# Key pages of a paged decode cache: strips of 32 partitions and block transposes on VectorE, two sequences per score

## The chip, the cores and the metric

The kernel runs on one core of a Trainium2 chip. The metric is the device time of one execution in microseconds (us), the median of several runs; lower is better. The engines are named as in the profile: PE (TensorE, its weight loads as PEld), DVE (VectorE), ACT (ScalarE), POOL (GpSimd) and SP (SyncE, which here only issues DMAs). PSUM is the memory that PE writes, in eight banks of 512 float32 per partition.

## What is computed

One step of a two-layer decoder, all in float32: a prompt of 1,024 new positions, and 8 sequences that add 4 positions each to a cache of 4,096 past positions. Layer A mixes by a convolution module, layer B by stick-breaking attention; each ends in a gated feed-forward network. The change touches the attention alone:

```python
z = jnp.einsum('bqhd,bkhd->bhqk', qb, kb) * scale + bias_f
causal = s_pos[None, :] < t_pos[:, None]
log_one_minus = jnp.where(causal, jax.nn.log_sigmoid(-z), 0.0)
after = lax.cumsum(log_one_minus, axis=3, reverse=True) - log_one_minus
w = jnp.where(causal, jnp.exp(jax.nn.log_sigmoid(z) + after), 0.0)
o = jnp.einsum('bhqk,bkhd->bqhd', w, vb)
...
past_k = cache_k[page_table].reshape(bs, -1, N_HEADS, HEAD_DIM)
past_v = cache_v[page_table].reshape(bs, -1, N_HEADS, HEAD_DIM)
```

There are 16 heads of 64. The weight of a key is sigmoid(z) times the product of sigmoid(-z) over all later keys, so keys are taken from the newest to the oldest and a running product ("remainder") is carried. A page holds 128 positions of all heads: 512 KB of keys and 512 KB of values. The 8 sequences have 32 pages each, 256 in all, scattered over a pool and named by a table.

## The kernel before

The stages follow one another: layer A, its feed-forward network, keys, values and queries of the new positions, the attention stage (`mix_sp`, `mix_pe`, `mix_act`, `mix_dve`, `mask_pool`, lines 2151 to 2622), then the output projection and the second feed-forward network. Weight tiles stream from HBM through three buffers (`raw`); ACT and DVE split each into a high and a low part (`split_hi` L369, `split_lo` L374), and PE makes three products per block (L1146).

The attention stage is a loop of 132 phases, written out by hand for each engine; semaphores tie the engines together. In phase p of the first 128:

- Two key pages are turned. SP loads each as 128 partitions (positions) by 1,024 columns (head, feature) of 4 KB into a ring of six (`kr`, L2197). PE turns every page in eight 128x128 transposes (L2262) into two PSUM banks of the four `TURN_BANKS`; ACT copies one half to `kt` (L2432), DVE the other (L2519). `kt` then has 128 rows (two heads of 64 features) for each of eight head pairs.
- In every odd phase a chunk of four pages (`CP = 4`, 512 positions of one sequence) is scored: eight products of 512 columns (L2275) from `kt` and the queries `qst`, which stand at places of their own among zeros. A sequence has 16 heads x 4 queries = 64 rows of the 128. ACT makes the two sigmoids (L2438, L2443), DVE the running product (`page_remainders`, a scan of 512, L2530) and the weights (`page_weights`, L2539). Three phases after the scoring PE turns the weights (L2284) and, a phase later, multiplies them with the value pages (`page_outputs`, L2298), which SP loads into a ring of six (`vr`).
- In three phases of four a unit of the prompt's own attention goes through the same steps for one pair of heads, 128 queries and up to 512 keys: scores (L2317), sigmoids (L2460, L2470), scan (L2564), mask on POOL (L2188), weights (`prompt_weights`, a product on DVE, L2576), transposes (L2327) and values (L2336). Seven of the eight pairs are scored in three products of rounded high and low parts (made by `pair_high` on ACT and `pair_low` on POOL, L2177), the first pair in one float32 product. Keys, queries and values of a pair come by three DMAs (`load_pair`, L2223 to L2225) every 16 phases.

SP's program in the loop alternates: read a page number from the table (`value_load`, L2193), wait until the ring has a free place, issue the key page; the same for a value page eight pages behind (`V_LAG`). A place in `kr` is free when PE has turned the page (`s_th`), one in `vr` when PE has summed it (`s_pv`). In the last phases PE makes six of the eight blocks of the first output-projection tile (`attention_product`, L1301) between other work.

## Time and profile before

| | us |
|---|---|
| median of 3 runs | 3069.11 |
| lowest and highest run | 3067.57, 3071.78 |
| the profiled execution, its own time | 3068.7 |
| its span, first to last instruction | 3067.0 |
| attention stage, first page transpose to last | 1449.8 to 2174.4 |

The profile is one execution. Busy time of an engine is the time in which it has an instruction under way; idle time is put down to what ended it. "PEclk" or the granted clock is 1.00 at the full level (2.4 GHz) and 0.50 at the lower (1.2 GHz). "DMA share" is the time that the packets of all 16 DMA engines took, over 16 times the stretch, each packet booked where it starts, so that it can pass 1; GB/s are their bytes. GB/s divided by the share is what the engines move when all are busy.

### The profile page before, as it was taken

What the parts mean: (1) busy time and instruction counts of PE and PEld (TensorE: products, weight loads), DVE (VectorE), ACT (ScalarE), POOL (GpSimd) and SP (SyncE); (2) the same over time, 40 slices, a digit from 0 to 9 for tenths busy, and PEclk for the clock granted to TensorE, in tenths of its full rate; (3) what the DMA queues carried; (4) which work ended last, traced back from release to release, by engine and by line L of the source; (5) the groups of instructions that cost most, each with busy time, mean ns of one, the idle gap of its engine ahead of it and who ended that gap; (6) DMA issues with size and microseconds to landing.
All of it is one profiled execution on the core that took longest, in us unless ns stands there. A gap on an engine that the chain in (4) does not pass through costs nothing. (4 is left out here: it accounts for less than half of the span.)

```text
span 3067.0 us, 60298 instructions
## 1 busy us (share of the span) xinstructions
PE 3028.2 (99%) x23786; PEld 2606.3 (85%) x23786; DVE 1983.1 (65%) x2953; ACT 1387.2 (45%) x2363; POOL 251.7 (8%) x412
## 2 busy tenths in 40 slices
PE   8999999999999999999999999999999999999998
PEld 7987888888999998998666777676788888999998
DVE  6998677745655345534878888878667763565522
ACT  5444633333333333323777777777543333333322
POOL 0212000000000002221111111111000000000000
PEclk9999999999999999999999999999999999999999
DMA  4222233334333335647999999999633333333332
GB/s 131 76 82 79 82 96 96 96 107 120 103 91 90 97 104 184 192 146 228 356 391 384 383 386 383 392 394 376 233 102 96 97 95 112 111 110 90 88 107 86
DMA packets 483243, 534.49 MB, mean 174 GB/s; under 512 B 22241, under 2 KB 400474, under 8 KB 482888
## 3 DMA queue, kind: packets, MB, share of 16 engines
q1 hardware_dynamic: 467254, 482.90, 46.8%
q0 software_dynamic: 15616, 47.55, 4.6%
q8 instruction: 190, 3.11, 0.4%
q14 instruction: 91, 0.75, 0.1%
q10 hardware_dynamic: 92, 0.19, 0.0%
HBM read 486.84 MB, written 33.89 MB: 170 GB/s over the span
## 5 line engine op out<-in xcount | busy, mean ns | idle before, releaser
L377 DVE TENSOR_TENSOR wlo<-raw,whi 128x1024 fp32r<-128x1024 f32 (+1 forms) x368 | 441.9, 1201 | 556.7 <-ACT whi L372 543.4
L372 ACT CAST whi<-raw 128x1024 fp32r<-128x1024 f32 (+1 forms) x368 | 379.5, 1031 | 916.7 <-PE PS L1146 878.5
L1146 PE MATMUL PS<-xfh,whi 128*128 128x512 f32 (+2 forms) x2240 | 618.8, 327 | 1.2 <-DVE wlo L377 0.9
L1146 PE MATMUL PS<-xfh,wlo 128*128 128x512 f32 (+2 forms) x2240 | 615.1, 326 | 0.0
L1146 PE MATMUL PS<-xfl,whi 128*128 128x512 f32 (+2 forms) x2240 | 613.5, 325 | 0.0
L1146 PEld LDWEIGHTS PS<-xfh,whi 128*128 128x128 f32 x2240 | 379.0, 188 | 35.9 <-issue 3.8
L1146 PEld LDWEIGHTS PS<-xfl,whi 128*128 128x128 f32 x2240 | 379.7, 188 | 32.3 <-issue 0.5
L1146 PEld LDWEIGHTS PS<-xfh,wlo 128*128 128x128 f32 x2240 | 378.4, 188 | 32.8
L2262 PE MATMUL PS<-ident,kr 128*128 128x128 f32 x2048 | 276.9, 276 | 2.3 <-ACT kt L2432 2.3
L2262 PEld LDWEIGHTS PS<-ident,kr 128*128 128x128 f32 x2048 | 225.5, 140 | 50.3 <-issue 49.4
L2519 DVE COPY kt<-PS 128x512 f32<-128x512 f32 x256 | 169.1, 675 | 87.2 <-PE PS L2262 85.3
L1146 PE MATMUL PS<-pZ,whi 128*128 128x512 f32 x640 | 197.4, 390 | 0.0
L1601 DVE TENSOR_SCALAR cv<-gx,fT 128x512 f32<-128x512 f32 (+1 forms) x132 | 49.4, 402 | 197.2 <-issue 190.6
L1146 PE MATMUL PS<-pA,whi 128*128 128x272 f32 x1024 | 171.4, 289 | 0.0
L2432 ACT COPY kt<-PS 128x512 f32<-128x512 f32 x256 | 152.4, 596 | 40.7 <-PE PS L2262 38.9
L1146 PEld LDWEIGHTS PS<-pA,whi 128*128 128x128 f32 x1024 | 145.0, 188 | 0.6 <-issue 0.5
L1605 DVE SCALAR_TENSOR_TENSOR cv<-gx,fT,cv 128x512 f32<-128x512 f32 (+1 forms) x264 | 142.4, 581 | 3.1
L1146 PEld LDWEIGHTS PS<-pZ,whi 128*128 128x128 f32 x640 | 120.1, 188 | 24.9
L1543 ACT ACTIVATE gel<-cv 128x512 f32<-128x512 f32 (+1 forms) x88 | 56.8, 646 | 183.5 <-DVEq L1612 183.4
L949 DVE SCALAR_TENSOR_TENSOR mT<-u,vec,mT 128x513 f32<-128x513 f32 (+1 forms) x203 | 135.9, 746 | 4.3 <-ACT mT L856 4.3
L2298 PE MATMUL PS<-vr,wT 128*32 128x256 f32 x2048 | 136.8, 385 | 1.5 <-DVE PS L2587 1.5
L2275 PE MATMUL PS<-kt,qst 128*32 128x512 f32 x1024 | 123.1, 595 | 7.7 <-issue 6.3
(379 smaller groups left out, 5311.3 us busy)
## 6 DMA issues: line engine op xcount, KB each, us to landing
kr<-in_cache_k SPq DMA_DIRECT2D x256, 512.0 KB, 6.7
vr<-in_cache_v SPq DMA_DIRECT2D x256, 512.0 KB, 6.4
raw<-in_ffn_w_gate SPq DMA_DIRECT2D x88, 512.0 KB, 3.7
raw<-in_ffn_w_up SPq DMA_DIRECT2D x88, 512.0 KB, 3.7
raw<-in_ffn_w_down SPq DMA_DIRECT2D x64, 512.0 KB, 3.9
raw<-in_ffn_w_down SPq DMA_DIRECT2D x32, 384.0 KB, 3.5
raw<-in_conv_w_glu SPq DMA_DIRECT2D x16, 512.0 KB, 4.0
raw<-in_conv_w_out SPq DMA_DIRECT2D x16, 512.0 KB, 3.9
```

The source lines that it names most:

```text
L372: nc.scalar.copy(whi[b][:, 0:blocks_of(t), :], raw[t % RAWS][:, 0:blocks_of(t), :]).then_inc(w_hi, 1)
L377: nc.vector.tensor_tensor(wlo[t % RAWS][:, 0:n, :], raw[t % RAWS][:, 0:n, :], whi[b][:, 0:n, :].bitcast(F32), ALU.subtract).then_inc(w_lo, 1)
L949: glu_then(nc.vector.scalar_tensor_tensor(out=d, in0=src, scalar=w, in1=d, op0=ALU.mult, op1=ALU.add))
L1146: mm = nc.tensor.matmul(PS[:, s + c, 0:c1 - c0], stationary(wt, t, kw + k), x(k0 + k)[:, c0:c1], start=start and k == 0 and wt is whi and ...
L1543: nc.scalar.activation(gel[:, 0:w], cv[0][:, 0:w], ACT.Gelu_apprx_tanh).then_inc(f_gel, 1)
L1601: then(nc.vector.tensor_scalar(a_, win(0), tap, None, ALU.mult))
L1605: then(nc.vector.scalar_tensor_tensor(out=d, in0=win(j), scalar=tap, in1=s_, op0=ALU.mult, op1=ALU.add))
L2262: mm = nc.tensor.transpose(PS[:, bank, j * P:(j + 1) * P], kr[slot][:, a * P:(a + 1) * P], ident[:])
L2275: mm = nc.tensor.matmul(PS[32 * g:32 * g + 32, 2, :], qst[:, c // SEQ_CHUNKS, a, :], kt[:, a, :], start=e == 0, stop=e == 1, skip_group_ch ...
L2298: mm = nc.tensor.matmul(PS[32 * g:32 * g + 32, 3, 0:256], wT[c % 2][:, m, 32 * g:32 * g + 32], vr[slot][:, 256 * g:256 * g + 256], start=F ...
L2432: nc.scalar.copy(kt[:, 0:4, m * P:(m + 1) * P], PS[:, turn_bank("page", x, 0), :].rearrange("p (a s) -> p a s", a=4)).then_inc(s_ka, 1)
L2519: nc.vector.tensor_copy(kt[:, 4:8, m * P:(m + 1) * P], PS[:, turn_bank("page", x, 1), :].rearrange("p (a s) -> p a s", a=4)).then_inc(s_kd, 1)
```

## The change

Key pages are no longer turned by PE. Two pages at a time, one of each of two sequences, are loaded in strips: for each page two DMAs (`f` = 0, 1), each with half of the features (512 columns) into 32 partitions, as four rows of 2 KB per partition. The four strips of a step fill 128 partitions. DVE then turns the step in two instructions of 1,024 elements, in 32x32 blocks, from `kr` straight to `kt`. `kt` has 32 rows for each of (feature half f, sequence z), and 16 blocks; a chunk is two steps (`CP = 2`), 256 positions of two sequences, so scores have 128 useful rows: sixteen products of 256 columns instead of eight of 512. There are still 64 chunks, 256 pages and 128 phases; scans, sigmoids and weights of a chunk are 256 wide instead of 512.

Also: the prompt's weight product moves from DVE to POOL; all prompt pairs are scored in one float32 product, so `pair_high` and `pair_low` go; the prompt's outputs have bank 7 to themselves and `TURN_BANKS` are three; the new positions' keys and queries come by eight strip DMAs and are put in place by 20 small copies (before: two DMAs, four copies); the first output-projection tiles are split after the loop, and none of their blocks is made inside it.

```diff
-KR, VR = 6, 6
+KT, VR = 3, 6
-CP = 4
+CP = 2
+DP = DB // 2
+SC = CP * PAGE
...
+    kr = [stack(f"kr{j}", [P, 4, 512]) for j in range(KT)]
...
-    sp.dma_start(kTs[:], k_dram[:, :, NP:T].rearrange("a p t -> p a t")).then_inc(s_in, 16)
-    sp.dma_start(qTs[:], q_dram[:, :, NP:T].rearrange("a p t -> p a t")).then_inc(s_in, 16)
+    for raw_, dram in ((kraw, k_dram), (qraw, q_dram)):
+        for q0 in range(4):
+            f = q0 // 2
+            src = dram[4 * f:4 * f + 4, :, NP:T].rearrange("a (j n) t -> n (a j) t", n=32)
+            sp.dma_start(raw_[32 * q0:32 * q0 + 32, :, :], src).then_inc(s_in, 16)
...
 def mask_pool(pool):
     for u, (pr, i, kc) in enumerate(ATT):
...
+            pool.wait_ge(a_r, 2 * u + hh + 1)
+            if u >= 1:
+                pool.wait_ge(t_full, turns["prompt", u - 1, hh] + 1)
+            nc.gpsimd.tensor_tensor(wq[hh][:, 0:w], beta[hh][:, 0:w], rem[hh][:, c0 + 1:c0 + 1 + w], ALU.mult).then_inc(a_w, 1)
...
-def load_page(sp, x, cache, ring, landed, freed, each):
-    number = sp.value_load(ptab[0:1, page_entry(x):page_entry(x) + 1], min_val=0, max_val=cache.shape[0] - 1)
-    slot = x % len(ring)
-    if x >= len(ring):
-        sp.wait_ge(freed, each * (x - len(ring) + 1))
-    sp.dma_start(ring[slot][:], cache[ds(number, 1)].rearrange("a s h d -> (a s) (h d)")).then_inc(landed[slot], 16)
+def load_k_page(sp, x):
+    number, step, z = page_number(sp, x, A["cache_k"]), x // 2, x % 2
+    if step >= KT:
+        sp.wait_ge(s_th, 2 * (step - KT + 1))
+    page = A["cache_k"][ds(number, 1)].rearrange("a s h d -> (a s) (h d)")
+    for f in range(2):
+        q0 = 64 * f + 32 * z
+        sp.dma_start(kr[step % KT][q0:q0 + 32, :, :],
+                     page[:, 512 * f:512 * f + 512].rearrange("(c r) n -> r c n", c=4)).then_inc(s_k[step % KT], 16)
...
 def page_scores(c):
-    pe.wait_ge(s_ka, CP * (c + 1))
-    pe.wait_ge(s_kd, CP * (c + 1))
+    pe.wait_ge(s_th, 4 * c + 4)
...
-    for e in range(2):
+    for i in range(4):
         for g in range(4):
-            a = 2 * g + e
-            mm = nc.tensor.matmul(PS[32 * g:32 * g + 32, 2, :], qst[:, c // SEQ_CHUNKS, a, :], kt[:, a, :],
-                                  start=e == 0, stop=e == 1, skip_group_check=True)
+            mm = nc.tensor.matmul(PS[32 * g:32 * g + 32, 2, 0:SC], qst[:, c // SEQ_CHUNKS, 4 * g + i, :], kt[:, 4 * g + i, :],
+                                  start=i == 0, stop=i == 3, skip_group_check=True)
...
-    terms = ((qp, kp),) if pr == 0 else ((qh, kh), (qh, kl), (ql, kh))
...
 for p in range(PHASES):
-    if pages:
-        page_half_turned(pages[0], 0)
     if turned is not None:
         prompt_weights_turned(turned, 0)
-    if pages:
-        page_half_turned(pages[0], 1)
     if summed is not None:
         page_weights_turned(summed)
-    if pages:
-        page_half_turned(pages[1], 0)
-        page_half_turned(pages[1], 1)
...
-    if p >= PHASES - 4 and p < PHASES - 1:
-        j = p - PHASES + 4
-        attention_product(pe, 0, 2 * j, 2 * j + 2)
...
-attention_product(pe, 0, 6, KB)
+attention_product(pe, 0, 0, KB)
...
+def page_turned(p, h):
+    c, m, slot = p // CP, p % CP, p % KT
+    if h == 0:
+        dve.wait_ge(s_k[slot], 64 * (p // KT + 1))
+        if c >= 1 and m == 0:
+            dve.wait_ge(s_sc, c)
+    nc.vector.transpose(bass.AP(kt, m * P + 64 * h, [(16 * SC, P), (32, 2), (SC, 16), (1, 32)]),
+                        kr[slot][:, 2 * h:2 * h + 2, :].rearrange("p c (j n) -> p c j n", n=32)).then_inc(s_th, 1)
```

How the order moves, at the two places that matter. SP in the middle of the loop, one key page and the value page after it, before (`ISA` rows are register arithmetic and waits, `TENSOR_LOAD ptab` reads the page number):

```order
L2193 TENSOR_LOAD ptab
L2193 ISA x2
L2197 ISA [waits smp_k_half_turned]
L2197 DMA kr_177<-in_cache_k 128x1024
L2193 TENSOR_LOAD ptab
L2193 ISA x2
L2197 ISA [waits smp_v_summed]
L2197 DMA vr_181<-in_cache_v 128x1024
```

and with the change:

```order
L2196 TENSOR_LOAD ptab
L2196 ISA x2
L2205 ISA [waits smp_k_half_turned]
L2205 DMA kr_178<-in_cache_k 32x4x512
L2205 ISA
L2205 DMA kr_178<-in_cache_k 32x4x512
L2196 TENSOR_LOAD ptab
L2196 ISA x2
L2212 ISA [waits smp_v_summed]
L2212 DMA vr_181<-in_cache_v 128x1024
```

A key page now takes two DMAs with one step of register arithmetic between them; the value page and the page-number reads stand as before, and the wait for a free place now asks for DVE's transposes instead of PE's.

DVE in the same place, two phases before (page copies, the prompt's weights `wq`, the chunk's scan and weights, the prompt's scans `rem`; the scans print as SCALAR_TENSOR_TENSOR here):

```order
L2519 COPY kt<-PS 128x4x128 [waits smp_k_half_turned] x2
L2576 TENSOR_TENSOR wq_192<-beta_190,rem_167 128x256 [waits att_gate_masked,weights_in_turn_bank,att_gates,att_remainders]
L2576 TENSOR_TENSOR wq_193<-beta_191,rem_168 128x256 [waits att_gate_masked,weights_in_turn_bank,att_gates,att_remainders]
L2564 SCALAR_TENSOR_TENSOR rem_167<-rest_188,rem_167,zero 128x512 [waits att_remainders,att_weights,att_gates]
L2564 SCALAR_TENSOR_TENSOR rem_168<-rest_189,rem_168,zero 128x512 [waits att_remainders,att_weights,att_gates]
L2519 COPY kt<-PS 128x4x128 [waits smp_scored,smp_k_half_turned]
L2526 COPY rems<-rems 128x1 [waits smp_weights]
L2530 SCALAR_TENSOR_TENSOR rems<-rests,rems,zero 128x512 [waits smp_remainders,smp_gates,smp_remainder_carried]
L2519 COPY kt<-PS 128x4x128 [waits smp_k_half_turned]
L2576 TENSOR_TENSOR wq_192<-beta_190,rem_167 128x512 [waits weights_in_turn_bank,att_gates,att_remainders]
L2576 TENSOR_TENSOR wq_193<-beta_191,rem_168 128x512 [waits weights_in_turn_bank,att_gates,att_remainders]
L2539 TENSOR_TENSOR ws<-betas,rems 128x512 [waits weights_in_turn_bank,smp_gates,smp_remainders]
```

and with the change:

```order
L2474 STREAM_TRANSPOSE kt<-kr_176 128x2x16x32 [waits smp_scored,k_pages_landed0]
L2482 COPY rems<-rems 128x1 [waits smp_weights]
L2486 SCALAR_TENSOR_TENSOR rems<-rests,rems,zero 128x256 [waits smp_remainders,smp_gates,smp_remainder_carried]
L2474 STREAM_TRANSPOSE kt<-kr_176 128x2x16x32
L2495 TENSOR_TENSOR ws<-betas,rems 128x256 [waits weights_in_turn_bank,smp_gates,smp_remainders]
L2520 SCALAR_TENSOR_TENSOR rem_169<-rest_189,rem_169,zero 128x512 [waits att_remainders,att_weights,att_gates]
L2520 SCALAR_TENSOR_TENSOR rem_170<-rest_190,rem_170,zero 128x512 [waits att_remainders,att_weights,att_gates]
L2474 STREAM_TRANSPOSE kt<-kr_177 128x2x16x32 [waits k_pages_landed1]
L2474 STREAM_TRANSPOSE kt<-kr_177 128x2x16x32
```

The two copies of a phase have become two transposes of 1,024 elements, the first of which waits for the strips to land; the `wq` products have left the engine, and the chunk's scan and weights are half as wide.

## Rows read from the trace of the kernel before

**Rows 1.** Busy time of the engines over the span (the page, part 1): us, share, instructions.

```profile
PE 3028.2 (99%) x23786; PEld 2606.3 (85%) x23786; DVE 1983.1 (65%) x2953; ACT 1387.2 (45%) x2363; POOL 251.7 (8%) x412
```

**Rows 2.** Waits of SP and PE, 1450 to 2150 us: us in total, times, longest.

```profile
SPq L2197 <- PE PS L2298: 95.6, 58, 2.8
SPq L2197 <- PE PS L2262: 28.3, 31, 2.2
...
PE PS L2262 <- ACT kt L2432: 1.8, 9, 0.3
```

**Rows 3.** Mid-stage window: us, busy PE, PEld, DVE, ACT, POOL, clock, DMA share, GB/s.

```profile
1500.00:2100.00 600.00, 592.66 (x7308) 421.48 (x7306) 491.06 (x729) 441.86 (x856) 94.90 (x117) 1.00 1.01 385
```

**Rows 4.** The page transposes of PE: duration min/median/max, first and last start.

```profile
L2262 PE MATMUL PS<-ident,kr x2048: 270/273/330, 1449.8 to 2174.4; 128*128 128x128 f32 x187
```

**Rows 5.** DMAs at work: whole pages, 512-byte weight pieces, strips.

```profile
1722.00:1724.00 2.00, 2.00 (x20) 1.91 (x18) 1.56 (x2) 2.00 (x5) 0.00 (x0) 1.00 1.03 418
2500.00:2700.00 200.00, 200.00 (x1076) 174.52 (x1075) 100.25 (x145) 69.37 (x95) 6.48 (x12) 1.00 0.36 109
62.40:62.60 0.20, 0.20 (x3) 0.20 (x2) 0.20 (x1) 0.20 (x2) 0.20 (x1) 1.00 1.07 241
64.40:64.60 0.20, 0.20 (x4) 0.20 (x2) 0.00 (x0) 0.20 (x3) 0.20 (x1) 1.00 1.47 285
62.00:69.00 7.00, 7.00 (x46) 7.00 (x45) 2.62 (x4) 7.00 (x31) 3.33 (x7) 1.00 0.60 155
```

**Rows 6.** The strips of rows 5 (DMA issues): count, KB each, us to landing.

```profile
shifted<-mT SPq DMA_DIRECT2D x56, 65.5 KB, 2.8
```

**Rows 7.** Groups by line, 1250 to 2200 us: xcount | busy us, mean ns | idle before.

```profile
L2262 PE MATMUL PS<-ident,kr 128*128 128x128 f32 x2048 | 276.9, 276 | 2.3 <-ACT kt L2432 2.3
L2519 DVE COPY kt<-PS 128x512 f32<-128x512 f32 x256 | 169.1, 675 | 87.2 <-PE PS L2262 85.3 <-POOL later L2171 1.9
L2530 DVE TENSOR_TENSOR_SCAN rems<-rests,rems,zero 128x512 f32<-128x512 f32 x64 | 100.6, 1571 | 2.7 <-ACT rests L2438 1.6
L2576 DVE TENSOR_TENSOR wq<-beta,rem 128x128 f32<-128x128 f32 (+3 forms) x192 | 97.4, 547 | 0.0
L377 DVE TENSOR_TENSOR wlo<-raw,whi 128x1024 fp32r<-128x1024 f32 x35 | 42.9, 1225 | 119.2 <-ACT whi L372 119.2
L2539 DVE TENSOR_TENSOR ws<-betas,rems 128x512 f32<-128x512 f32 x64 | 43.6, 681 | 0.7 <-ACT betas L2443 0.7
L2317 PE MATMUL PS<-k_high,q_high 64*128 64x512 f32 (+2 forms) x168 | 37.2, 439 | 0.0
L2317 PE MATMUL PS<-k_low,q_high 64*128 64x512 f32 (+2 forms) x168 | 29.1, 344 | 0.0
L2317 PE MATMUL PS<-k_high,q_low 64*128 64x512 f32 (+2 forms) x168 | 29.0, 342 | 0.0
L2317 PE MATMUL PS<-kp,qp 64*128 64x512 f32 (+3 forms) x48 | 11.0, 535 | 0.0
L2188 POOL TENSOR_SCALAR_AFFINE_SELECT beta<-beta 128x128 f32<-128x128 f32 x128 | 77.2, 616 | 467.4 <-ACT beta L2470 466.2
L2177 POOL TENSOR_TENSOR k_low<-kp,k_high 128x1024 fp32r<-128x1024 f32 x7 | 16.6, 2368 | 94.9 <-ACT k_high L2414 94.9
```

**Rows 8.** SP's queue in mid-stage, page after page: start us, us.

```profile
1702.10 0.34 SPq L2197 DMA_DIRECT2D vr<-in_cache_v  x1
1703.20 0.34 SPq L2197 DMA_DIRECT2D kr<-in_cache_k  x1
```

**Rows 9.** SP's queue where DMAs follow without a page number: start us, us.

```profile
1463.92 0.42 SPq L2224 DMA_DIRECT2D qp<-q_feature_major  x1
1464.39 0.43 SPq L2225 DMA_DIRECT2D vp<-out  x1
```

**Rows 10.** The chunk's scan on DVE: duration min/median/max.

```profile
L2530 DVE TENSOR_TENSOR_SCAN rems<-rests,rems,zero x64: 1268/1284/2897, 1459.7 to 2178.9; 128x512 f32<-128x512 f32 x64
```

**Rows 11.** Products of the projections on PE (the page, part 5).

```profile
L1146 PE MATMUL PS<-xfh,whi 128*128 128x512 f32 (+2 forms) x2240 | 618.8, 327 | 1.2 <-DVE wlo L377 0.9
```

More of the change, by code:

```diff
@@ L238, in yoco_step @@
     rs_x = at("rs_x", [P, NH], F32, small[0])
-    om = tiny("om", [P, 256])
+    spare = tiny("spare", [P, 256])
     oc = tiny("oc", [P, DB, HD])
@@ L2097, in chunk_scored, with turn_bank_read @@
             return p // 2 if p >= 0 and p % 2 == 1 and p // 2 < NCH else None
-        turns, turn_order = {}, []
+        turns = {}
         for p in range(PHASES):
-            pages, unit, chunk = pages_turned(p), unit_scored(p - 2), chunk_scored(p - 3)
-            order = [("page", pages[0], 0)] if pages else []
+            unit, chunk = unit_scored(p - 2), chunk_scored(p - 3)
             if unit is not None:
-                order.append(("prompt", unit, 0))
-            if pages:
-                order.append(("page", pages[0], 1))
+                turns["prompt", unit, 0] = len(turns)
             if chunk is not None:
-                order.append(("pages", chunk))
-            if pages:
-                order += [("page", pages[1], 0), ("page", pages[1], 1)]
+                turns["pages", chunk] = len(turns)
             if unit is not None:
-                order.append(("prompt", unit, 1))
-            for task in order:
-                if task[0] != "page":
-                    turns[task] = len(turns)
-                turn_order.append(task)
-        TURN_BANKS = (0, 1, 6, 7)
-        turn_at = {task: n for n, task in enumerate(turn_order)}
-        def turn_bank(*task):
-            return TURN_BANKS[turn_at[task] % 4]
+                turns["prompt", unit, 1] = len(turns)
+        TURN_BANKS = (0, 1, 6)
+        def turn_bank(*task):
+            return TURN_BANKS[turns[task] % 3]
+        def turn_bank_read(pe, *task):
+            n = turns[task]
+            if n < 3:
+                set_read(pe, 0)
+            else:
+                pe.wait_ge(t_read, n - 2)
         def tile_pairs(u):
@@ L2172, in att_pool @@
                                     pattern=[[-1, P]], channel_multiplier=1).then_inc(a_mk, 1)
[L2174 to L2177 removed]
         def mask_pool(pool):
             for u, (pr, i, kc) in enumerate(ATT):
[L2181 to L2186 removed]
+                w, c0 = keys_of(i, kc), r_col(i, kc)
+                for hh in range(2):
+                    pool.wait_ge(a_sg, 4 * u + hh + 3)
+                    if is_diag(i, kc):
                         t = beta[hh][:, w - P:w]
@@ L2230, in mix_sp @@
                 mix_values_sp(sp, x)
-            for x in range(KR, NPG + V_LAG):
+            for x in range(2 * KT, NPG + V_LAG):
                 mix_pages_sp(sp, x)
@@ L2402, in attention_block_free @@
             if k == 3:
-                eng.wait_ge(s_pv, PAGES * (DB - 1) + 1)
+                eng.wait_ge(s_pv, PAIR_PAGES * (DP - 1) + 1)
             if k >= 3:
-                eng.wait_ge(s_th, 2 * NPG)
-        PAIR_AT = {16 * pr - 16 + p: (pr, j) for pr in range(1, PAIRS) for j, p in enumerate((7, 11))}
-        def pair_high(act, pr, j):
-            b = pr % 2
-            act.wait_ge(a_ld[b], 48 * (pr // 2 + 1))
-            if pr >= 2:
-                act.wait_ge(a_pv, PER_PAIR * (pr - 1))
-            nc.scalar.copy((kh, qh)[j][b][:], (kp, qp)[j][b][:]).then_inc(pair_rounded, 1)
+                eng.wait_ge(s_th, NPG)
         def attention_high(act, k):
@@ L2426, in mix_act @@
         def mix_act(act):
-            def page_copied(x):
-                c, m = x // CP, x % CP
-                act.wait_ge(s_th, 2 * x + 1)
-                if c >= 1 and m == 0:
-                    act.wait_ge(s_sc, c)
-                nc.scalar.copy(kt[:, 0:4, m * P:(m + 1) * P], PS[:, turn_bank("page", x, 0), :].rearrange("p (a s) -> p a s", a=4)).then_inc(s_ka, 1)
             def page_rests(c):
@@ L2600, in mix_dve @@
                     prompt_finished(unit_scored(p - 3))
-                if done and done[1] % PAGES == PAGES - 1:
-                    own_heads(done[1] // PAGES)
+                if done and done[1] % PAIR_PAGES == PAIR_PAGES - 1:
+                    own_heads(done[1] // PAIR_PAGES)
                 if pages:
-                    page_copied(pages[0])
+                    page_turned(p, 0)
                 if scored is not None:
@@ L2607, in mix_dve @@
                 if pages:
-                    page_copied(pages[1])
-                if unit_scored(p - 1) is not None:
-                    for hh in range(2):
-                        prompt_weights(unit_scored(p - 1), hh)
+                    page_turned(p, 1)
                 if scored is not None:
@@ L2736, in _ @@
                         smp_in_sp(sp)
-                    if half == 1 and n >= 1 and n < 1 + KR:
+                    if half == 1 and n >= 1 and n < 1 + 2 * KT:
                         mix_pages_sp(sp, n - 1)
@@ L2742, in _ @@
             mix_sp(sp)
-            sp.wait_ge(s_w, NCH)
-            assert (first["out10"] + 2) % RAWS == ATT_RAW
+            sp.wait_ge(a_z, NU)
+            assert first["out10"] % RAWS == 0
             out_sp(sp, 1, 0, 2)
```

339 lines of the change are left out of this document (145 added, 194 removed).

## The prediction

> **What bounds the kernel now.** I read the busy shares first, then the waits of the attention stage, then its stretches by DMA traffic, because the change is confined to that stage. PE is busy for 99% of the span [rows 1]. In the stage it hardly waits: 1.8 us for the page copies in 700 us, and no row of PE names a DMA, while SP does wait for PE, 95.6 + 28.3 us, until PE gives back a place in a ring [rows 2]. So PE sets the pace and the loads follow it. But they follow closely: from 1500 to 2100 us PE is busy for 592.66 of 600 us, and the DMA share is 1.01 at 385 GB/s [rows 3]. The two limits lie side by side, and whatever is taken from PE can only be won down to what the DMA engines need. The first page transpose starts at 1449.8 us, the last at 2174.4 [rows 4]; that is 127 phases and the 2.1 us that the last phase's own sixteen transposes take, so **5.69 us a phase**.
>
> **What the DMA engines need per phase.** A phase loads two key pages and two value pages, 1.049 MB of each, and 0.098 MB of the prompt's pairs (three 512 KB loads in 16 phases). GB/s over share is the rate with all engines busy: 418 / 1.03 = 406 GB/s for whole pages, whose pieces are 4 KB; 109 / 0.36 = 303 GB/s for the weights' 512-byte pieces [rows 5]. A piece so takes an engine 161 ns or 27 ns, and a straight line between them gives 85 ns for 2 KB, 387 GB/s. Before: 2 x 2.58 + 0.26 (pairs, at some 380 GB/s) = 5.43 us, 95% of the phase.
>
> **The strips are the term that decides.** A key DMA now writes 32 partitions, not 128. The kernel already has such DMAs, the shifted copies of layer A: 32 partitions by 2,096 bytes, 65.5 KB each [rows 6]. While they alone are under way the rate at full share is far lower: 241 / 1.07 = 225 GB/s in one stretch with every engine busy, 285 / 1.47 = 194 in another, 155 / 0.60 = 258 over the whole burst [rows 5]. They have strips at both ends and in SBUF, the change has strips only where it writes, and each of its DMAs is four times as long. No row shows a strip load from HBM. I take 225 GB/s: the pieces are of nearly the same size, and the engines are all busy there, as they are in the stage; 194 and 258 are the near bounds, 387 (a strip costs nothing) is the far one. Keys: 1.049 MB / 225 = 4.66 us. With 2.58 for values and 0.26 for pairs a phase needs **7.50 us**, 1.81 more than now: 128 x 1.81 = **+232 us**. At 258 it is 6.90 (+155), at 194 it is 8.25 (+328), at 387 it is 5.55 (-17).
>
> By the Trainium skill (SBUF — State Buffer, "Door 1: The DMA port swizzle") 32 partitions reach 8 of the 16 ports into SBUF, and 1 MiB moves at 189 GB/s against 328 for 128 partitions; two DMAs to the two halves, side by side, gain 6% ("Can I just issue two DMAs to hit both halves?"). That holds for loads from HBM, which our row does not show. An estimate by this page is 406 x 189/328 x 1.06 = 248 GB/s, a phase of 7.07 us, and a total of 3250; I keep the row.
>
> **The other engines, per phase.**
> - PE now has 592.66/600 x 5.69 = 5.62 us. The 2,048 transposes (276.9 us [rows 7], 2.16 a phase) go. The prompt's three products cost 95.3 us for 84 units, 1.13 each, the single product 11.0 for 12 units, 0.92 [rows 7]: 0.1 a phase goes. Scores keep their columns, 16 x 256 for 8 x 512. Left: 3.3 us, hidden under 7.50. The granted clock is 1.00 in every row of the stage; at the lower level of 1.2 GHz throughout 3.3 us would be 6.6, still hidden.
> - DVE has 491.06/600 x 5.69 = 4.66. Out go the copies (169.1 us, 1.32 a phase), `wq` (97.4, 0.76), half of the chunk's scan (100.6, so 0.39) and half of `ws` (43.6, 0.17) [rows 7], leaving 2.02. In come two transposes of 1,024 elements. No row shows one; nearest is the split of 1,024 float32 on DVE, 1,225 ns [rows 7], which is of the same size and from SBUF to SBUF. The dear bound is the scan's rate, 512 in 1,284 ns [rows 10], so 2.57 us; the cheap one is 0.68, a copy of half the size [rows 7]. With 1.23 the phase has 4.5 us, between the bounds 3.4 to 7.2; all hide. The new wait is the first transpose's, for the strips: behind it on DVE stand the chunk's scan and weights and the prompt's scans, and behind these PE, ACT and POOL, so the whole phase follows the loads.
> - POOL gets `wq`: 576 elements a phase on average, at the 2,368 ns for 1,024 of its own product [rows 7] 1.33 us, beside 77.2/128 = 0.60 of masks, and loses `pair_low`. Some 1.9 us. A product on POOL and a scan on DVE may hold each other up: the scan has a median of 1,284 ns but a longest of 2,897 [rows 10]. Even in turn, 4.5 + 1.9 is 6.4.
> - ACT only loses work (page copies, half of the chunk's sigmoids, `pair_high`).
> - SP issues a page every 1.10 us when it need not wait [rows 8]; a DMA without a page number follows after 0.47 [rows 9]. Four pages and two more DMAs: 4.40 + 0.94 + 0.1 for the pairs = 5.44 us, under 7.50. Behind its wait for a key place stands the next value page; that wait now ends with DVE's transposes of three steps before, and while strips land late it is DVE that waits, not SP.
> - Ahead of the stage twelve key DMAs stand for six and nine small loads for three, 12 more at 0.47 between weight loads, and 16 more tiny copies on DVE; the queue of two weight tiles covers them. Uncovered it is 6 us.
> - Behind it, the 18 products of `attention_product` that stood in the last phases come after the loop: 18 x 0.276 (618.8 us for 2,240 [rows 11]) = **+5 us**. The later split of the first output tile lies beside the last value products.
>
> **The sum.** The profiled execution took 3068.7 us, 0.4 less than the median of the runs shown. 3068.7 + 232 + 5 = 3305.7; with the 0.4, **3306 us**.
>
> **The rivals.**
> 1. *Strips cost nothing (faster).* The sixteen DMA engines drift apart, so that some write one strip while others write another or a value page, and they no longer hold each other up: 5.55 us a phase, 3068.7 - 17 + 5 = 3057 us. It decides if the strips move above 373 GB/s, where the phase is short by the 5 us of the end. For it: long DMAs, and value pages between. Against it: the bursts of rows 5 with two queues at once stayed under 260. The Trainium skill (DMA: Bandwidth & Descriptors, "Specifications") asks of a piece only 512 bytes for the full rate; by that the keys would take 2.58 and the total would be 3041, but rows 5 show 303 against 406 GB/s at that size.
> 2. *No change.* Strips cost nothing, but SP (5.44) and DVE and POOL in turn come so near to the phase that the few waits fill it to 5.69: 3069 + 5 = 3074, or less by what of the 5 us stays hidden.
> 3. *SP's queue becomes the bound.* If the second strip costs SP as much as a page, 1.10: 6.60 + 0.1 = 6.70, +129 + 5 = 3203 us. Against it: 0.47 [rows 9].
> 4. *DVE becomes the bound.* Transposes at 2.57 and POOL's products in turn: 7.2 + 1.3 = 8.5, +360 + 5 = 3434.
>
> That the change does not do what it says is excluded: the order shows the strips, the transposes, and no page transposes on PE.
>
> **Chances.** The forecast 0.63, rival 1 0.15, rival 2 0.09, rival 3 0.08, rival 4 0.05. A measurement of this kernel tells 0.2%, 6 us, from no change. Rival 1 is faster, rival 2 the same, the others slower: 0.15, 0.09, 0.76. The forecast's own range is 3180 (strips at 285 GB/s, half way in time from 225 to 387, if the value pages between them help: 3.68 + 2.58 + 0.26 = 6.52 a phase) to 3405 (194 GB/s). Without rivals 1 and 4 and the forecast's tails more than 2 in 10 would be left out, so the range reaches down to rival 1, 3055, and up to 3410; rival 4 and the tails are outside.
>
> **What would show it.** Right: in mid-stage a DMA share near 1.0 at 270 to 320 GB/s; key DMAs landing later than the 6 to 7 us of now; DVE's first transpose of a phase, and behind it PE's scores, waiting for the key strips; transposes near 1.2 us; PE busy for about half of the stage. Wrong: 375 GB/s or more in the stage (rival 1 or 2); strips issued more than 0.6 us apart on SP with the DMA share well below 1 (rival 3); DVE busy throughout with landed strips waiting for it (rival 4).

## The result and the profile after

The change makes the kernel **slower: 3499.88 us median (3477.31 to 3503.81, 4 runs)** against 3069.13 for before in the same runs, a ratio of 1.1389 with a 95% interval of 1.1362 to 1.1416: 431 us more, where 237 were forecast. The time lies above the stated range. The direction and the kind of the cause hold; one term of the sum was far too small.

The profiled execution of after: span 3495.1 us, against 3067.0 before. Its stage runs from 1459.9 to 2591.9 us, by the two lines of the key transposes: DVE's in the view by source line, and busy time over the span from the page.

```profile
PE 2984.4 (85%) x22468; PEld 2443.8 (70%) x22468; DVE 1962.9 (56%) x2764; ACT 1198.7 (34%) x2093; POOL 375.6 (11%) x588
...
L2474 DVE STREAM_TRANSPOSE kt<-kr x256: 1196/1221/1246, 1459.9 to 2591.9; 128x1024 f32<-128x1024 f32 x128
```

From the start of the first transpose to the start of the last it is 1132.0 us. Without some 1.5 us between the two transposes of the last phase, these are 127 phases of **8.90 us** each, where before took 5.69 [rows 4] and 7.50 was forecast. The stage accounts for 407 of the 428 us that the span grew (1132.0 against 724.6).

The window of the mid-stage of after (us, busy PE, PEld, DVE, ACT, POOL, granted clock, DMA share, GB/s):

```profile
1500.00:2500.00 1000.00, 585.72 (x6453) 301.19 (x6456) 486.69 (x580) 296.62 (x657) 196.37 (x271) 0.75 1.04 241
```

Against [rows 3]: the DMA engines are as fully booked as before (share 1.04 for 1.01) and move 241 GB/s in place of 385. PE is down to 59%, DVE to 49%. The clock granted to PE is 0.75 on average, between its two levels, in a stretch in which PE stands still two fifths of the time. The longest waits of after from 1500 to 2500 us (us in total, times, longest), in place of [rows 2], where no wait of PE names a DMA:

```profile
ACT rests L2399 <- PE PS L2265: 504.4, 55, 12.4
DVE kt L2474 <- DMA kr<-in_cache_k: 479.1, 109, 12.4
PE PS L2288 <- DMA vr<-in_cache_v: 408.1, 158, 8.7
```

DVE waits 479 us for strips, as forecast, and PE waits **408 us for value pages**, which the forecast does not have at all: it says that the phase follows the key loads. The DMA issues of the whole run of after (count, KB each, us to landing) say the same:

```profile
kr<-in_cache_k SPq DMA_DIRECT2D x512, 256.0 KB, 11.9
vr<-in_cache_v SPq DMA_DIRECT2D x256, 512.0 KB, 18.9
```

A value page is loaded exactly as before, and now lands 19 us after its issue instead of 6.8 (median from 1600 to 2000 us before). The trace also holds the pieces (packets) that the DMA engines moved. The table counts those that start from 1600 to 2000 us. A piece of 2,048 bytes is a row of a strip or of half a page; one of 4,096 is a row of a whole page or of a prompt pair (in e4, which loads no value pages there, of pairs alone):

```
                      2,048 bytes             4,096 bytes
                   count  median  mean     count  median  mean   (ns)
before                 -                   36992   159    169
after              21959   147    149      11745   267    268
e1_spread2k        35051    84     88      18557   159    173
e2_stride4         29998    84     95      15752   159    191
e3_rows64          22811   144    144      12170   266    264
e4_no_values       38686   141    138       1280   164    195
e5_one_dma             -                   39069   159    163
e6_batched         23307   146    143      12188   194    218
e7_same_side       20402   160    162      10963   292    290
e9_two_queues      22834   136    141      12188   252    262
e10_before_halves      -                   22889   279    278
e11_before_columns 34592    84     89      18314   159    173
```

The row of after is the result: a strip's row takes 147 ns, which is what 225 GB/s means (2,048 x 16 / 225 = 146). The value rows, priced at 161 ns, take 267. Per phase the strips are 512 rows on 16 engines, 512/16 x 149 = 4.8 us, the values 256/16 x 268 = 4.3, the pairs 0.26: 9.3 us of DMA time, in a stretch booked at a share of 1.04, hence 8.9.

The parts that were moved between engines, after, from 1250 to 2650 us:

```profile
L2474 DVE STREAM_TRANSPOSE kt<-kr 128x1024 f32<-128x1024 f32 x256 | 309.3, 1227 | 516.0 <-DMA kr<-in_cache_k 508.7 <-PE PS L2265 5.5 <-issue 1.9
L2486 DVE TENSOR_TENSOR_SCAN rems<-rests,rems,zero 128x256 f32<-128x256 f32 x64 | 47.5, 742 | 5.8 <-ACT rests L2399 4.7
L2495 DVE TENSOR_TENSOR ws<-betas,rems 128x256 f32<-128x256 f32 x64 | 24.7, 386 | 0.3 <-ACT betas L2404 0.3
...
L2193 POOL TENSOR_TENSOR wq<-beta,rem 128x128 f32<-128x128 f32 (+3 forms) x192 | 199.0, 1043 | 610.9 <-PE PS L2313 343.1 <-DVE rem L2520 211.0 <-issue 51.5
```

A transpose costs 1,227 ns (forecast 1.23 us); the chunk's scan and weights take about half of their means in [rows 7] (742 for 1571 ns, 386 for 681); POOL's product is 199.0 / 128 = 1.55 us a phase (1.33).

### The profile page after: what moved, and what is told of

It is laid out like the page before. It is cut to its first block, busy times and chain, and to the rows that moved or that the text cites. A ratio compares the mean times of both kernels' runs of the same rounds, so it can differ in the third digit from the quotient of the medians.

```text
span 3495.1 us, 57750 instructions
## 1 busy us (share of the span) xinstructions
PE 2984.4 (85%) x22468; PEld 2443.8 (70%) x22468; DVE 1962.9 (56%) x2764; ACT 1198.7 (34%) x2093; POOL 375.6 (11%) x588
## 4 chain that ended last, share of the span: by engine, by line
PE 57%; DMA 20%; DVE 9%; SPq 8%; issue 4%; ACT 2%; DVEq 0%; POOL 0%; ACTq 0%; POOLq 0%
PE PS L1150 52%; DMA kr<-in_cache_k 14%; DMA vr<-in_cache_v 5%; SPq L2205 4%; DVE mT L953 3%; DVE kt L2474 1%; SPq L2196 1%; SPq L2212 1%; DVE wlo L381 1%; PE PS L2265 1%; ACT whi L376 1%; PE PS L670 1%; PE PS L1801 0%; PE PS L1023 0%; PE PS L714 0%
## 5 line engine op out<-in xcount | busy, mean ns | idle before, releaser
L2474 DVE STREAM_TRANSPOSE kt<-kr 128x1024 f32<-128x1024 f32 x256 | 309.3, 1227 | 516.0 <-DMA kr<-in_cache_k 508.7
L2288 PE MATMUL PS<-vr,wT 128*32 128x256 f32 x2048 | 202.9, 477 | 458.2 <-DMA vr<-in_cache_v 444.3
L2288 PEld LDWEIGHTS PS<-vr,wT 128*32 128x32 f32 x2048 | 47.1, 119 | 591.6 <-DMA vr<-in_cache_v 353.7
L2193 POOL TENSOR_TENSOR wq<-beta,rem 128x128 f32<-128x128 f32 (+3 forms) x192 | 199.0, 1043 | 610.9 <-PE PS L2313 343.1
L2399 ACT ACTIVATE rests<-PS,nb 128x256 f32<-128x256 f32 x64 | 30.3, 473 | 564.2 <-PE PS L2265 564.2
L2265 PE MATMUL PS<-kt,qst 128*32 128x256 f32 x2048 | 204.2, 568 | 8.9 <-DVE kt L2474 8.9
L2265 PEld LDWEIGHTS PS<-kt,qst 128*32 128x32 f32 x2048 | 92.3, 164 | 107.7 <-issue 78.4
L2421 ACT ACTIVATE rest<-PS,nsb 128x128 f32<-128x128 f32 (+3 forms) x192 | 103.0, 584 | 101.6 <-PE PS L2303 66.9
```

The source lines that it names most:

```text
L2193: nc.gpsimd.tensor_tensor(wq[hh][:, 0:w], beta[hh][:, 0:w], rem[hh][:, c0 + 1:c0 + 1 + w], ALU.mult).then_inc(a_w, 1)
L2265: mm = nc.tensor.matmul(PS[32 * g:32 * g + 32, 2, 0:SC], qst[:, c // SEQ_CHUNKS, 4 * g + i, :], kt[:, 4 * g + i, :], start=i == 0, stop=i ...
L2288: mm = nc.tensor.matmul(PS[32 * g:32 * g + 32, 3, 256 * z:256 * z + 256], wT[step // CP % 2][:, step % CP, 32 * g:32 * g + 32], bass.AP(vr ...
L2421: nc.scalar.activation(rest[hh][:, 0:w], PS[:, 4 + hh, 0:w], ACT.Sigmoid, bias=nsb[:, h:h + 1], scale=-1.0).then_inc(a_sg, 1)
L2474: nc.vector.transpose(bass.AP(kt, m * P + 64 * h, [(16 * SC, P), (32, 2), (SC, 16), (1, 32)]), kr[slot][:, 2 * h:2 * h + 2, :].rearrange(" ...
```

## The experiments

Two theories stood at the start. **A**: the narrow landing does it, for the strips and for whatever is under way with them; A1 if it is 32 (or more) *neighbouring* partitions that share few ways into SBUF, A2 if it is the small number of partitions in a DMA. **B**: it is the 2 KB pieces read at 4 KB spacing and the doubled number of DMAs. All times below are against before in the same runs; the phase is worked out as above, for e10 and e11, which turn their pages on PE, as for before.

| run | us | ratio to before | 95% interval | us a phase |
|---|---|---|---|---|
| after | 3499.88 | 1.1389 | 1.1362 to 1.1416 | 8.90 |
| e1_spread2k | 3092.85 | 1.0078 | 1.0049 to 1.0107 | 5.79 |
| e2_stride4 | 3219.01 | 1.0489 | 1.0459 to 1.0520 | 6.77 |
| e3_rows64 | 3495.76 | 1.1391 | 1.1323 to 1.1458 | 8.88 |
| e4_no_values | 3033.69 | 0.9885 | 0.9857 to 0.9914 | 5.35 |
| e5_one_dma | 3046.84 | 0.9927 | 0.9907 to 0.9947 | 5.44 |
| e6_batched | 3466.13 | 1.1294 | 1.1271 to 1.1316 | 8.74 |
| e7_same_side | 3572.19 | 1.1639 | 1.1569 to 1.1709 | 9.63 |
| e8_before_single | 3070.50 | 1.0004 | 0.9995 to 1.0014 | - |
| e9_two_queues | 3472.70 | 1.1313 | 1.1280 to 1.1345 | 8.80 |
| e10_before_halves | 3483.05 | 1.1346 | 1.1309 to 1.1384 | 8.91 |
| e11_before_columns | 3085.15 | 1.0048 | 1.0026 to 1.0071 | 5.83 |

### e1: the same pieces, spread over 128 partitions

```diff
-                q0 = 64 * f + 32 * z
-                sp.dma_start(kr[step % KT][q0:q0 + 32, :, :],
-                             page[:, 512 * f:512 * f + 512].rearrange("(c r) n -> r c n", c=4)).then_inc(s_k[step % KT], 16)
+                sp.dma_start(kr[step % KT][:, 2 * z + f, :],
+                             page[:, 512 * f:512 * f + 512]).then_inc(s_k[step % KT], 16)
```

> The kernel after, with each key DMA writing its 512 columns into all 128 partitions (one 2 KB row each) instead of 32 partitions (four rows each); same number of DMAs, same pieces, same reads. The keys then stand in the wrong places, so the scores are of other numbers; the work is the same. A phase of the kernel after takes 8.88 us (first to last key transpose 1132.0 us). Theory A (the narrow landing of a strip slows both the strips and the value pages under way with them): key pieces back near 85 ns, value pieces back from 263 to 159 ns, a phase of 5.5 to 5.9 us, total 3050 to 3115 us. Theory B (the 2 KB pieces read at 4 KB spacing, or twice the DMAs, cost it, and where they land is indifferent): unchanged, 3480 to 3505 us.

3092.85 us. Theory A: 407 us of the loss go with the landing alone; the reads, the pieces and the number of DMAs are unchanged. The window of e1 and its SP queue, page after page (start us, us):

```profile
1600.00:2000.00 400.00, 300.63 (x4042) 163.59 (x4044) 308.08 (x367) 186.22 (x411) 132.74 (x172) 0.91 1.02 377
```

```profile
1800.59 0.85 SPq L2204 DMA_DIRECT2D kr<-in_cache_k  x2
1802.20 0.34 SPq L2211 DMA_DIRECT2D vr<-in_cache_v  x1
1803.30 0.85 SPq L2204 DMA_DIRECT2D kr<-in_cache_k  x2
```

Value rows are back at 159 ns although nothing was done to them: that they were slow was the strips' doing. SP issues a key and a value page every 2.71 us without a pause, 5.4 a phase, which is the 5.44 forecast for its queue. The DMA engines are full beside it: by the table a phase needs 512/16 x 88 + 256/16 x 173 ns + 0.26 us = 5.85 us of them. The phase is 5.79, so this run does not say which of the two bounds it.

### e2: 32 partitions, four apart

```diff
-                q0 = 64 * f + 32 * z
-                sp.dma_start(kr[step % KT][q0:q0 + 32, :, :],
+                sp.dma_start(bass.AP(kr[step % KT], 2048 * (2 * f + z), [(2048 * 4, 32), (512, 4), (1, 512)]),
```

> The kernel after, with a strip's 32 partitions four apart (over the whole of the 128) instead of side by side; still 32 partitions and four 2 KB rows each in a DMA. The keys stand in the wrong places, so the scores are of other numbers. 
3219.01 us, between the two, but the pieces decide: 84 and 159 ns at the median, as in e1. So 32 partitions are enough if they are not neighbours: A1. What is left over fits SP. The key DMAs of SP by source line (duration min/median/max in ns), e1 and then e2:

```profile
L2204 SPq DMA_DIRECT2D kr<-in_cache_k x512: 332/337/3089, 1397.4 to 2183.1; - x171
```

```profile
L2204 SPq DMA_DIRECT2D kr<-in_cache_k x512: 602/613/3046, 1398.7 to 2313.8; - x171
```

A key DMA here occupies SP for 613 ns instead of 337: 512 x 0.276 = 141 us, about the 126 by which e2 exceeds e1. The window agrees: its DMA share falls to 0.94.

```profile
1600.00:2000.00 400.00, 282.56 (x3514) 153.14 (x3510) 266.28 (x317) 158.71 (x351) 112.69 (x145) 0.84 0.94 321
```

That the spacing of the partitions makes the DMA dear for SP is not shown: in e3, with neighbouring partitions, the median is 610 ns.

### e3: 64 neighbouring partitions

```diff
-                q0 = 64 * f + 32 * z
-                sp.dma_start(kr[step % KT][q0:q0 + 32, :, :],
-                             page[:, 512 * f:512 * f + 512].rearrange("(c r) n -> r c n", c=4)).then_inc(s_k[step % KT], 16)
+                sp.dma_start(kr[step % KT][64 * f:64 * f + 64, 2 * z:2 * z + 2, :],
+                             page[:, 512 * f:512 * f + 512].rearrange("(c r) n -> r c n", c=2)).then_inc(s_k[step % KT], 16)
```

> The kernel after, with each key DMA in 64 neighbouring partitions (two 2 KB rows each; the first DMA of a page in the lower half, the second in the upper). The keys stand in the wrong places, so the scores are of other numbers. Theory A2 (few partitions in a DMA): half of the loss goes, 3260 to 3320 us. Theory A1 in its plain form (share of the 128 partitions reached) says the same; in the form of the Trainium skill (SBUF - State Buffer, Door 1: The DMA port swizzle), by which 64 neighbouring partitions reach no more ports than 32, unchanged: 3470 to 3510 us.

3495.76 us: twice the partitions, and nothing won (SP's 610 ns are not the reason, as e2 with 613 runs at 6.77 us a phase). A2 falls, and so does A1 in the form "share of the 128 partitions". Its window is that of after:

```profile
1600.00:2000.00 400.00, 228.78 (x2605) 118.78 (x2606) 200.40 (x240) 121.12 (x265) 81.20 (x110) 0.76 1.05 247
```

### e4: no value pages

```diff
         def load_v_page(sp, x):
+            if x >= VR:
+                return
             number, slot = page_number(sp, x, A["cache_v"]), x % VR
-            if x >= VR:
-                sp.wait_ge(s_pv, x - VR + 1)
...
-                pe.wait_ge(s_v[slot], 16 * (x // VR + 1))
+                pe.wait_ge(s_v[slot], 16)
```

> The kernel after without the value loads but the first six: the value products take the six pages that are there again and again, so the output is of other values. Strips then move alone but for the prompt's pairs. If strips have a price of their own (about 147 ns for 2 KB, as in the kernel after and as the prediction took it): 4.7 + 0.26 = 5.0 us a phase, total 2980 to 3030 us. If strips were slow only because value pages were under way with them (85 ns): the DMAs need 3.0 us and DVE's 4.5 us a phase would bound it, 2920 to 2960 us.

3033.69 us, a little above the first case. The total alone does not decide between the cases, because the transfers do not set the pace here (DMA share 0.92); the rows do. Strips alone take 138 ns a row on average (141 at the median), 4.4 us a phase: most of the price is their own. The window and the longest waits of the computing engines behind ACT's:

```profile
1600.00:2000.00 400.00, 316.06 (x4482) 179.33 (x4472) 342.24 (x409) 203.15 (x454) 149.86 (x191) 0.94 0.92 220
```

```profile
PEld PS L2265 <- DVE kt L2474: 78.5, 38, 3.7
POOL wq L2193 <- DVE rem L2520: 71.4, 19, 8.3
PE PS L2265 <- DVE kt L2474: 64.1, 36, 3.5
```

Among the long waits of this run there is none for a transfer. What holds the phase at 5.35 us is DVE (busy 342 of 400 us, 4.6 a phase) and PE waiting for each other: one engine's sum, 4.5, was not the whole bound.

### e5: a key page by one DMA

```diff
-            for f in range(2):
-                q0 = 64 * f + 32 * z
-                sp.dma_start(kr[step % KT][q0:q0 + 32, :, :],
-                             page[:, 512 * f:512 * f + 512].rearrange("(c r) n -> r c n", c=4)).then_inc(s_k[step % KT], 16)
+            sp.dma_start(kr[step % KT][:, 2 * z:2 * z + 2, :],
+                         page.rearrange("r (c n) -> r c n", c=2)).then_inc(s_k[step % KT], 16)
...
-                    dve.wait_ge(s_k[slot], 64 * (p // KT + 1))
+                    dve.wait_ge(s_k[slot], 32 * (p // KT + 1))
```

> The kernel after, with each key page loaded by one DMA as a value page is: 128 partitions of 4 KB. The keys stand in the wrong places, so the scores are of other numbers. The spread run (e1) took 3092.9 us, 5.8 us a phase, with SP's queue issuing without a pause every 2.73 us for a key and a value page. If SP's second DMA was what bounded e1: SP now needs 4.5 us a phase, the DMA engines 5.6 to 5.7 (168 ns a piece on average, as in the kernel before), the other engines 5.34 (e4): total 3065 to 3080 us. If the 2 KB pieces or the computing engines bounded e1: 3085 to 3100 us.

3046.84 us, 0.7% faster than before, and below the 3065 expected: with whole pages the mean row costs 163 ns, not the 168 that I carried over. What bounded e1 stays open, because this edit takes away SP's second DMA and the 2 KB pieces together. The rows alone would account for it: 512/16 x 163 ns = 5.2 us for keys and values, 0.37 less than in e1, where the phase is 0.35 shorter. The phase of 5.44 us is the floor that the prediction named, 5.43, and the window shows full engines; the computing engines' 5.35 (e4) lie just under it:

```profile
1600.00:2000.00 400.00, 313.36 (x4390) 173.78 (x4391) 333.40 (x399) 197.74 (x441) 142.79 (x185) 0.93 1.03 407
```

This is the worth of all the rest of the change, if keys could land in 128 partitions: 22 us. The strips cost 3499.9 - 3046.8 = 453, of which 407 go with the landing alone (e1).

### e6: eight strips, then four value pages

```diff
-                mix_pages_sp(sp, x)
+                if x % 4 == 2:
+                    for y in range(x, min(x + 4, NPG)):
+                        load_k_page(sp, y)
+                    for y in range(max(x - V_LAG, VR), min(x + 4 - V_LAG, NPG)):
+                        load_v_page(sp, y)
```

> The kernel after, with SP's queue in another order: eight strips (four key pages), then four value pages, instead of two strips and one value page in turn. Computes the same as after. If value pages are slow only while strips are under way beside them (in the kernel after 263 ns a piece against 159 to 173 without strips), coarser turns separate them: strips 4.4 us a phase as alone (e4), values 2.8, pairs 0.26, so about 7.5 us, total 3300 to 3350 us, or part of the way there. If order does not matter: 3480 to 3510 us.

3466.13 us: the direction is right (value rows fall from 267 to 194 ns at the median), the size is not, 34 us for the 150 to 200 expected. Coarser turns in the queue keep strips and values apart only in part, and another wait takes over. From 1600 to 2000 us DVE's wait for strips falls from 192.4 to 9.1 us, but PE still waits for value pages (173.0 us in after), SP waits more for a free key place (36.8 in after), and the DMA share falls to 0.97:

```profile
PE PS L2292 <- DMA vr<-in_cache_v: 164.4, 44, 14.1
SPq L2205 <- DVE kt L2478: 99.0, 37, 5.8
```

### e7: the two strips of a page side by side

```diff
-                q0 = 64 * f + 32 * z
+                q0 = 32 * f + 64 * z
```

> The kernel after, with the two strips of a page in neighbouring 32-partition groups (0 and 32, then 64 and 96) instead of 64 apart (0 and 64, then 32 and 96). The keys stand in the wrong places, so the scores are of other numbers. If the two strips of a page move side by side and groups 64 apart do not disturb each other, while neighbours do: slower than after, the key strips at about half of 406 GB/s, 203, in place of 221 to 237: 3530 to 3620 us. If only one strip moves at a time, or strips of different pages overlap as well: unchanged, 3480 to 3510 us.

3572.19 us, slower by 72, with strip rows at 160 ns for 147. This fits the first case: that the two strips of a page move side by side to some extent, and that groups 64 apart disturb each other less than neighbours. By the Trainium skill (SBUF — State Buffer, "Can I just issue two DMAs to hit both halves?") the gain of the two sides is 6% of a transfer's rate; here it is 9% of a strip row's time (the page compares two DMAs with one, this run two places of the second).

### e8: one part alone in the kernel before, the single prompt product

```diff
-                terms = ((qp, kp),) if pr == 0 else ((qh, kh), (qh, kl), (ql, kh))
+                terms = ((qp, kp),)
```

(with the rounding of pairs on ACT and POOL left out)

> The kernel before with one part of the change alone: the prompt's scores of all pairs in one float32 product, without the rounding of pairs on ACT and POOL. PE loses some 0.21 us for each of 84 units, 17.6 us. If PE bounds the kernel before: 3049 to 3056 us. If the DMA engines do as much (168 ns a piece on average, 5.65 of the phase's 5.69 us): 3062 to 3069 us, no change.

3070.50 us, no change, and it cannot tell what it was made for, because it takes nothing from PE. PE's timeline of before and then of this run, a unit of 512 keys (start us, us):

```profile
1802.82 0.51 PE L2317 MATMUL PS<-k_high,q_high 64*128 64x512 f32 x2
1803.16 0.40 PE L2317 MATMUL PS<-k_low,q_high 64*128 64x512 f32 x2
1803.40 0.40 PE L2317 MATMUL PS<-k_high,q_low 64*128 64x512 f32 x2
1803.73 1.07 PE L2298 MATMUL PS<-vr,wT 128*32 128x256 f32 x16
```

```profile
1800.82 1.13 PE L2313 MATMUL PS<-kp,qp 64*128 64x512 f32 x4
1801.88 1.07 PE L2296 MATMUL PS<-vr,wT 128*32 128x256 f32 x16
```

From start to start, three products take 0.91 us and the single one 1.06 (for a unit of 128 keys 0.48 and 0.42). The 0.21 us a unit came from busy times of matmuls that overlap.

### e9: the upper strips on a second queue

```diff
-            for f in range(2):
+            for f in range(2) if step < KT else (0,):
...
+            def upper_strips(step):
+                act.wait_ge(s_th, 2 * (step - KT + 1))
+                for z in range(2):
+                    number = page_number(act, 2 * step + z, A["cache_k"])
+                    page = A["cache_k"][ds(number, 1)].rearrange("a s h d -> (a s) (h d)")
+                    act.dma_start(kr[step % KT][64 + 32 * z:96 + 32 * z, :, :],
+                                  page[:, 512:1024].rearrange("(c r) n -> r c n", c=4)).then_inc(s_k[step % KT], 16)
...
+                if KT <= p + KT - 1 < NPG // 2:
+                    upper_strips(p + KT - 1)
```

> The kernel after, with the upper strip of each key page (partitions 64 and up) issued on ACT's queue, with page numbers that ACT reads itself, and the lower one on SP's as before. Computes the same. If strips are slow because one queue hands them out one after another, so that mostly one side of 64 partitions is written at a time: lower and upper strips now move side by side, pieces fall towards 84 and 160 ns, 3100 to 3300 us. If the queue has no part in it: 3440 to 3520 us. By the Trainium skill (SBUF - State Buffer, Can I just issue two DMAs to hit both halves?) issuing from several engines does not help, which is the second case.

3472.70 us, the second case: 27 us won, about as much as the runs of after lie apart. Strip rows take 136 ns, value rows 252 at the median. The waits move (from 1600 to 2000 us PE waits 4.8 us for value pages, 173.0 in after, and SP 192.6 for a free key place), but the window stays full at the low rate, and the phase with it at 8.80.

```profile
1600.00:2000.00 400.00, 223.28 (x2592) 117.38 (x2592) 206.61 (x238) 117.22 (x264) 84.26 (x110) 0.78 1.04 247
```

The Trainium skill (SBUF — State Buffer, "Can I just issue two DMAs to hit both halves?") says that issuing from several engines does not help; e9 agrees but for its 27 us in 3500.

### e10 and e11: the landing alone, in the kernel before

e10 (e11 takes `ring[slot][:, 512 * f:512 * f + 512]` and `page[:, 512 * f:512 * f + 512]` in the last line):

```diff
-            sp.dma_start(ring[slot][:], cache[ds(number, 1)].rearrange("a s h d -> (a s) (h d)")).then_inc(landed[slot], 16)
+            page = cache[ds(number, 1)].rearrange("a s h d -> (a s) (h d)")
+            if ring is vr:
+                sp.dma_start(ring[slot][:], page).then_inc(landed[slot], 16)
+            else:
+                for f in range(2):
+                    sp.dma_start(ring[slot][64 * f:64 * f + 64, :], page[64 * f:64 * f + 64, :]).then_inc(landed[slot], 16)
```

> The kernel before with one part of the change alone: each key page by two DMAs, each into 64 neighbouring partitions, in 4 KB pieces as before; everything else as before, and the same results. If narrow landing by itself slows keys and the value pages beside them, whatever the piece size and the computation (e3 was as slow with 64 partitions as the kernel after with 32): a phase of 8.5 to 9 us, 3430 to 3500 us. If the loss needs 2 KB pieces or the changed computation: 3069 to 3100 us.

> The kernel before with each key page by two DMAs of 128 partitions and 2 KB pieces (columns 0 to 511, then 512 to 1023); the same number of DMAs as in the run with halves, the same results. If only the landing counts: SP's queue needs 5.45 us a phase (e1), the DMA engines 5.85, so 3069 to 3100 us. If the second DMA or the smaller pieces cost it: as the run with halves.

3483.05 and 3085.15 us. One edit of the kernel before, which still turns its pages on PE, in 4 KB pieces, reproduces the loss: +414 of the +431 us. The same two DMAs per page cut by columns, so that each reaches all partitions, cost 16. The windows of e10 and e11:

```profile
1600.00:2000.00 400.00, 293.40 (x3005) 194.24 (x3008) 210.12 (x302) 185.78 (x352) 37.31 (x48) 0.87 1.03 240
```

```profile
1600.00:2000.00 400.00, 385.26 (x4712) 272.66 (x4714) 319.60 (x471) 285.49 (x550) 62.99 (x76) 0.99 1.01 372
```

In e10 key and value rows, alike in size, take 279 ns at the median, 240 GB/s with all engines full.

## Why the prediction was right and where it failed

- **What bounds before** (PE, with the DMA engines close behind): supported. With PE relieved and nothing else slow (e5) the phase falls from 5.69 to 5.44 us and stops at the DMA floor that was given as 5.43.
- **Strips decide**: right. 225 GB/s for strips, taken from the 2 KB strips of layer A [rows 5], was a good price: 147 ns a row in after, 138 alone in e4 (2,048 x 16 / 138 = 237 GB/s). That it fits so closely is partly luck: it was one of three stretches that gave 194 to 258, from SBUF to SBUF, and half of the bytes of that burst moved in pieces of 4,192 bytes, not 2,096.
- **The step that failed** is "With 2.58 for values and 0.26 for pairs a phase needs **7.50 us**". The sum added the price of strips under way alone to that of value pages under way alone. Both are under way together, and the value rows, loaded as before, take 267 ns for 161: 256/16 x (267 - 161) = 1.7 us a phase, 128 x 1.7 = 217 us, which is more than the 194 by which the forecast fell short (the row times sum to 9.3 us a phase, and at a share of 1.04 they take 8.9). The step behind it, that "the whole phase follows the loads" of keys, missed the second path: PE waits 408 of 1000 us for value pages. No bound of the range and no rival let the value pages become slower, so the range ended at 3410. e1 shows that the strips' landing makes the values slow (159 ns as soon as it is wide), e10 that this needs neither the strips' small pieces nor the new computation. That they get slower together than the sum of both alone (4.4 + 2.7 + 0.26 = 7.4 against 8.9) is shown; why they do is open, no run here separates it.
- **The estimate by the Trainium skill** (SBUF — State Buffer, "Door 1: The DMA port swizzle"), 248 GB/s for strips and 3250 us in total, missed by the same term: for the strips alone e4 shows 237 GB/s, near it, and the value pages were priced as if alone here too.
- **DVE, POOL, ACT**: right in size. DVE 486.69 / 1000 x 8.9 = 4.3 us a phase (4.5), POOL 1.86 (1.9), a transpose 1.227 us (1.23). POOL's sum is luck: its products take 1.55 us a phase for 1.33, its masks 39.5 / 128 = 0.31 for 0.60. And e4 shows a phase of 5.35 by the computing engines, not 4.5: waits between DVE and PE come on top of the busiest engine's sum.
- **PE** was put at 3.3 us a phase and was busy for 585.72 / 1000 x 8.9 = 5.2, at a granted clock of 0.75. In e5, at 0.93, it is 313.36 / 400 x 5.44 = 4.3, still more than 3.3 / 0.93 = 3.5. The sum took the transposes' busy time off the engine's; that it is too much because matmuls overlap, as in e8, is argued. PE has the slack in after, but these 4.3 us stand beside DVE's 4.6 in e4.
- **SP** at 5.44 us: right, e1 issues at 5.4 with no pause. Rival 3 priced the second strip too dear.
- **Rival 1** (3057 if strips cost nothing) names about what e5 then gives with whole pages, 3047; its own condition, strips above 373 GB/s, did not come about. **Rival 4** falls with the transposes at 1.23 us.
- **PE's 0.1 us a phase less for the prompt** was wrong (e8), at no cost, because PE has slack in after.
- **Ahead and behind**: 20.7 us together (first transpose 10.1 later, from the last one to the end 10.6 longer) where 5 were given. Ahead, "covered" was wrong; in e5 the first transpose is 8.5 later as well, so the strips are not the main reason, and what is stays open. PE lost time there that before did not. From 1400 to 1425 us, where e5 has PE busy for 23.12 us, before and then after:

```profile
1400.00:1425.00 25.00, 24.50 (x119) 20.39 (x119) 11.11 (x24) 8.73 (x11) 2.82 (x6) 1.00 0.84 252
```

```profile
1400.00:1425.00 25.00, 20.13 (x99) 16.80 (x98) 6.83 (x11) 7.18 (x9) 1.62 (x3) 0.94 0.85 195
```

  Behind, it is 1.8 us in e5, so most of the 10.6 goes with the strips; that it is the slow loads of the last phases is argued.
- **Arithmetic**: strips at 194 GB/s give 3402 us, not 3405; nothing hangs on it.

No version here that computes the same is clearly faster than before. e5 shows what it would have to do: whole pages into 128 partitions, and scores from keys that then stand in four groups of positions. That was not built; e5 puts its worth at some 22 us.

## What to carry to other kernels

Price a DMA by where it lands as well as by its bytes and pieces, and where the queues are full, price the transfers beside it at the same time: here a landing in neighbouring partitions slowed the wide value pages of the same stretch from 159 to 267 ns a row, so the durations of two transfers measured alone did not add up. Before a layout is built on loads into a group of neighbouring partitions, try that landing in the old kernel by one edit (e10): here it told 414 of the 431 us without any of the new computation. The durations of overlapping matmuls did not tell what one costs (e8); take it from start to start.

## What was not expected of the hardware

- Loads into 64 neighbouring partitions were as slow as into 32 (3495.76 and 3499.88 us), loads into 32 partitions four apart moved each row as fast as 128 partitions do (84 ns, for 147 in after). Each DMA held SP's queue for 613 ns there and 610 in e3, for 337 in e1 and 322 in after; which part of its form decides that is open.
- Value pages that land in all 128 partitions slow down from 159 to 267 ns a row when narrow loads are under way with them, and neither a coarser order (e6) nor a second queue (e9) gave back more than 34 us of 431.
